# One weight unit for both gate rows in the last mixer, a third buffer for the mLSTM weights, and the order of its heads moved

## What is computed

```python
# x: 512 tokens, ctx: 256 tokens, D = 1024; 4 retention heads, 4 mLSTM heads of 128
hc = modulate(rms_norm(ctx, norm1), csh1, csc1)
rk_c, rv_c, mk_c, mv_c, gates_c = ...hc @ w_in...      # only states come out of the context
st_f, st_b = states after ctx, forward and backward
hx = modulate(rms_norm(x, norm1), sh1, sc1)
rq, rk, rv, rg, mq, mk, mv, mo, mg, bg_ret, bg_ml = split(hx @ w_in)
ret = retention(rope(rq), rope(rk), rv), forward + backward, from the states
ml  = mLSTM(mq, mk, mv, gates mg + bias), forward + backward, from the states
y_ret = head_norm(ret) * silu(rg);  y_ml = head_norm(sigmoid(mo) * ml)
x = x + g1 * ((sigmoid(bg_ret)*(y_ret @ w_ret_up) + sigmoid(bg_ml)*(y_ml @ w_ml_up)) @ w_out)
```

## Time and profile before

| | us |
|---|---|
| median of 3 runs (lowest, highest) | 2866.57 (2865.85, 2868.82) |
| profiled execution, device time | 2866.88 |
| profiled execution, span | 2865.2 |
| busy in the span: PE, DVE, ACT | 2807.3, 1457.5, 984.2 |

### The profile page before, as it was taken

The page is one execution under the profiler, slowest core; times in us unless marked ns, Lnnn a source line. Parts: engine busy times, 40 slices in busy tenths (PEclk is TensorE's granted clock), DMA queues, the critical chain, the costliest instruction groups (busy, mean ns, idle before and its releaser), DMA issues. The chain is left out here.

```text
span 2865.2 us, 34079 instructions
## 1 busy us (share of the span) xinstructions
PE 2807.3 (98%) x13630; PEld 2326.4 (81%) x13630; DVE 1457.5 (51%) x1931; ACT 984.2 (34%) x1093; POOL 32.9 (1%) x68
## 2 busy tenths in 40 slices
PE   7999999999999999999999999999999899899998
PEld 6888887788888888888887888888888788788886
DVE  7774356467743677434444443435545543623333
ACT  4222237432222322224444322324434432422221
POOL 0000000000000000000000000000000000000000
PEclk9999999999999999999999999999999999999999
DMA  5332231134322343222121322224311122222222
GB/s 182 136 139 88 103 134 60 45 134 148 136 103 103 125 140 138 95 107 92 49 74 45 118 89 102 88 103 147 110 70 65 45 74 103 74 102 92 98 103 74
DMA packets 68128, 288.80 MB, mean 101 GB/s; under 512 B 9488, under 2 KB 30352, under 8 KB 38464
## 3 DMA queue, kind: packets, MB, share of 16 engines
q1 hardware_dynamic: 59520, 257.97, 25.6%
q0 software_dynamic: 7936, 29.23, 3.0%
q10 hardware_dynamic: 576, 0.23, 0.0%
HBM read 285.31 MB, written 2.10 MB: 100 GB/s over the span
## 5 line engine op out<-in xcount | busy, mean ns | idle before, releaser
L1019 DVE TENSOR_TENSOR sb_WL<-sb_RAW,sb_WH 128x2048 fp32r<-128x2048 f32 x242 | 554.4, 2291 | 762.1 <-ACT sb_WH L435 761.9
L1797 PE MATMUL PS<-sb_HH,sb_WH 128*128 128x512 f32 x2288 | 900.8, 394 | 13.1 <-DVE sb_HL L1035 9.2
L1798 PE MATMUL PS<-sb_HL,sb_WH 128*128 128x512 f32 x2288 | 892.7, 390 | 0.0
L1799 PE MATMUL PS<-sb_HH,sb_WL 128*128 128x512 f32 x2288 | 892.6, 390 | 0.0
L435 ACT ACTIVATE sb_WH<-sb_RAW 128x2048 fp32r<-128x2048 f32 x242 | 463.2, 1914 | 788.5 <-PE PS L1799 786.6
L1797 PEld LDWEIGHTS PS<-sb_HH,sb_WH 128*128 128x128 f32 x2288 | 431.2, 188 | 107.9 <-issue 18.7
L1798 PEld LDWEIGHTS PS<-sb_HL,sb_WH 128*128 128x128 f32 x2288 | 431.1, 188 | 91.5 <-issue 3.4
L1799 PEld LDWEIGHTS PS<-sb_HH,sb_WL 128*128 128x128 f32 x2288 | 430.9, 188 | 90.5
L1797 PE MATMUL PS<-ff_GH,sb_WH 128*128 128x512 f32 x880 | 342.5, 389 | 1.9 <-DVE sb_WL L1019 1.9
L1798 PE MATMUL PS<-ff_GL,sb_WH 128*128 128x512 f32 x880 | 342.4, 389 | 0.0
L1799 PE MATMUL PS<-ff_GH,sb_WL 128*128 128x512 f32 x880 | 342.4, 389 | 0.0
(11 more groups left out here) (350 smaller groups left out, 2544.8 us busy)
## 6 DMA issues: line engine op xcount, KB each, us to landing
sb_RAW<-in_weights SPq DMA_DIRECT2D x230, 1024.0 KB, 4.8
ff_ADAW<-in_w_ada POOLq DMA_DIRECT2D x48, 512.0 KB, 4.0
sb_RAW<-in_weights SPq DMA_DIRECT2D x22, 512.0 KB, 5.1
sb_XT<-in_x SPq DMA_DIRECT2D x4, 512.0 KB, 9.7
out_t<-sb_XT SPq DMA_DIRECT2D x4, 512.0 KB, 2.7
b_CT<-in_ctx POOLq DMA_DIRECT2D x1, 1024.0 KB, 5.3
sb_RAW<-in_weights SPq DMA_DIRECT2D x4, 256.0 KB, 4.3
hy_BD<-in_c_gates POOLq DMA_DIRECT2D x1, 512.0 KB, 3.3
```

The lines of the kernel that those rows point to most:

```text
L1019: dve.tensor_tensor(WL[slot][:, :], RAW[slot][:, :], f32(WH[slot][:, :]), ALU.subtract).then_inc(*T["w_lo"].up())
L1797: pe.matmul(out, wh, xh, start=start, stop=False)
L1798: pe.matmul(out, wh, xl, start=False, stop=False)
L1799: return pe.matmul(out, wl, xh, start=False, stop=stop)
```

## The change

**Gates.** The unit with the gate columns is there once (242 used units instead of 243; the array in DRAM keeps its size). Its visit comes after the eight context visits and makes both rows: 24 matmuls of 256 columns on the context into one bank, 24 of 512 columns on the sequence into the next one. `take` moves both out with four ACT instructions. With that the context visits are the first of the list, the norm's steps begin one visit earlier (k = 0 to 3), and the visit in retention head 0 is gone; heads 1 to 3 keep theirs.

**mLSTM.** A third buffer `W2` lies over the gate rows, which are dead by then. d = 0 keeps `W0`, d = 1 uses `W1` and `W2` in turn. `weights(k)` waits for the values of k - 2 only for d = 0, for those of k - 4 for d = 1, and for the `QW` of k - 2. Both gate rows of the next head are spread together, ACT makes both sets of weights before it takes the visit out of PSUM, and DVE's list is ordered anew (below).

```diff
@@ lists
-    ("cmg", "cgates", 1), ("crk", "ctok", 2), ("crv", "ctok", 2), ("cmk", "ctok", 2), ("cmv", "ctok", 2),
-    ("rk", "feat", 2), ("rq", "feat", 2), ("rv", "tok", 2), ("mg", "gates", 1), ("mk", "feat", 2), ...
+    ("crk", "ctok", 2), ("crv", "ctok", 2), ("cmk", "ctok", 2), ("cmv", "ctok", 2), ("mg", "gates", 1),
+    ("rk", "feat", 2), ("rq", "feat", 2), ("rv", "tok", 2), ("mk", "feat", 2), ...
@@ buffers
-        WM = (ml["W0"], ml["W1"])
+        def WM(k):
+            return ml["W0"] if k % 2 == 0 else mz["W2"] if k % 4 == 3 else ml["W1"]
@@ ACT
             def weights(k):
                 ...
                 if k >= 2:
-                    act.wait_ge(T["ml_num"].sem, k - 1)
+                    act.wait_ge(T["ml_qw"].sem, k - 1)
+                    free = k - 1 if d == 0 else k - 3
+                    if free > 0:
+                        act.wait_ge(T["ml_num"].sem, free)
                 ...
             for h in range(NH):
                 if h + 1 < NH:
                     weights(2 * h + 2)
+                    weights(2 * h + 3)
+                    own_weights(2 * h + 2)
                 take(V_ML + h)
+                if h + 1 < NH:
+                    own_weights(2 * h + 3)
                 prepare(V_ML + h + 1)
                 if h + 1 < NH:
-                    weights(2 * h + 3)
                     squares(h)
@@ DVE
+            inter(0, 0)
             for h in range(NH):
+                inter(h, 1)
+                weighted(h, 0)
+                weighted(h, 1)
+                if h:
+                    gated_out(h - 1)
+                    prepare(V_ML + h)
+                weighted(h, 2)
+                weighted(h, 3)
                 if h:
                     head_sums(h - 1)
                 ...
                 divided(h, 0)
                 if h + 1 < NH:
                     own_keys(2 * h + 2)
+                    own_keys(2 * h + 3)
+                    inter(h + 1, 0)
                     divided(h, 1)
-                    own_keys(2 * h + 3)
-                    gated_out(h)
-                    prepare(V_ML + h + 1)
@@ PE, retention and mLSTM
             for h in range(NH):
                 ret_scores(h, 0)
                 ret_scores(h, 1)
-                visit(V_RET + h)
+                if h:
+                    visit(V_RET + h - 1)
                 ...
             for h in range(NH):
                 if h:
-                    spread(2 * h + 1)
                     part(V_ML + h, 0)
                 ...
                 if h + 1 < NH:
                     spread(2 * h + 2)
+                    spread(2 * h + 3)
```

More of the change, by code:

```diff
@@ L366, in _ @@
             u1 = U_B2 + len(B2_UNITS)
-            with sp.Fori(0, (N_UNITS - u1) // 2) as i:
+            with sp.Fori(0, (N_USED - u1) // 2) as i:
                 for s in range(2):
                     sp.wait_ge(T["w_lo"].sem, 2 * i + (u1 + s - 1))
-                    load((u1 + s) % 2, 2 * i + (u1 + s))
+                    load((u1 + s) % 2, 2 * i + (u1 + s + 1))
             for t in range(0, KT, 2):
@@ L540, in group @@
                     for c in range(chunks):
-                        if not isinstance(i, int) or ahead < u0 + chunks * (2 * i + j) + c + 1 < N_UNITS:
+                        if not isinstance(i, int) or ahead < u0 + chunks * (2 * i + j) + c + 1 < N_USED:
                             split_at(u0, 2 * chunks, i, chunks * j + c + 1)
@@ L840, in take @@
                             last.then_inc(*T["rope_sw"].up())
-                elif name in ("cmg", "mg"):
+                elif name == "mg":
                     act.wait_ge(T["mlb_in"].sem, 1)
-                    lo, w = (0, SC) if name == "cmg" else (SC, S)
-                    act.activation(gr["IG"][0:36, lo:lo + w], PS[0:36, b, 0:w], ACT.Identity, bias=col("ml_b", 0, rows=36))
-                    last = act.activation(gr["FG"][0:36, lo:lo + w], PS[64:100, b, 0:w], ACT.Identity, bias=col("ml_b", 1, rows=100)[64:100, :])
+                    for lo, w, bank_ in ((0, SC, b), (SC, S, b + 1)):
+                        act.activation(gr["IG"][0:36, lo:lo + w], PS[0:36, bank_, 0:w], ACT.Identity, bias=col("ml_b", 0, rows=36))
+                        last = act.activation(gr["FG"][0:36, lo:lo + w], PS[64:100, bank_, 0:w], ACT.Identity, bias=col("ml_b", 1, rows=100)[64:100, :])
                 elif name == "rg":
@@ L1686, in head_sums, with inter, weighted @@
                     .then_inc(*T["hn_ss"].up())
-            for h in range(NH):
[L1689 to L1696, removed]
+            def inter(h, d_):
+                dve.wait_ge(T["ml_w"].sem, 2 * h + d_ + 1)
+                if h:
+                    dve.wait_ge(T["ml_num"].sem, 2 * h + d_ - 1)
+                dve.tensor_tensor(mw["QW"][:, d_, :], b2["MQ"][:, h, :], SQT[:, d_, :], ALU.mult).then_inc(*T["ml_qw"].up())
+            def weighted(h, j):
+                dve.wait_ge(T["ml_s"].sem, TB * h + j + 1)
+                for d_ in range(2):
+                    lo, hi = span(d_, j)
+                    w = WM(2 * h + d_)
+                    last = dve.tensor_tensor(w[:, j, lo:hi], PS[:, j % 2, lo:hi], w[:, j, lo:hi], ALU.mult)
+                last.then_inc(*T["ml_sm"].up())
+            inter(0, 0)
+            for h in range(NH):
+                inter(h, 1)
+                weighted(h, 0)
+                weighted(h, 1)
+                if h:
+                    gated_out(h - 1)
+                    prepare(V_ML + h)
+                weighted(h, 2)
+                weighted(h, 3)
                 if h:
                     head_sums(h - 1)
[L1699 to L1703, removed]
-                        last = dve.tensor_tensor(WM[d_][:, j, lo:hi], PS[:, j % 2, lo:hi], WM[d_][:, j, lo:hi], ALU.mult)
-                    last.then_inc(*T["ml_sm"].up())
-                    if j == 1:
-                        inter(1)
                 dve.wait_ge(T["ml_qw"].sem, 2 * h + 2)
@@ L1908, in project @@
                 pe.wait_ge(T["w_lo"].sem, u + 1)
[L1909 to L1912 removed]
+                if kind == "feat":
+                    last = feature_major(u % 2, HH, HL, (b, b + 1), ready=ready)
+                elif kind == "gates":
+                    if u >= U_B2:
+                        feature_major(u % 2, hc["HCH"], hc["HCL"], (b,), tokens=SC)
+                        b += 1
+                    last = feature_major(u % 2, HH, HL, (b,), ready=ready)
                 elif kind == "tok":
@@ L2263, in ml_values @@
                     for j in order:
-                        last = pe.matmul(out, WM[d][:, j, c], b2["MV"][:, j, h, :], start=False, stop=j == order[-1])
+                        last = pe.matmul(out, WM(k)[:, j, c], b2["MV"][:, j, h, :], start=False, stop=j == order[-1])
                 last.then_inc(*T["ml_num"].up())
```

66 lines of the change are left out of this document (33 added, 33 removed).

## The result

The changed kernel takes 2850.88 us in the median of 5 runs (2849.65 to 2852.73), the kernel before beside it 2868.13 (2865.85 to 2868.82, 5 runs). The ratio is 0.9945, its 95% interval 0.9934 to 0.9956: 17 us less. The forecast was 2852.1 in a range of 2848.7 to 2858.1. The profiled execution took 2852.57, 14.3 less than the profiled one of before; the sum said 14.5 less.

What follows compares the result with a forecast made beforehand. PE was taken as the bound (98% of the span), with only its waits and the half clock behind some to gain. -6.8 + 3.3 + 1.7 + 0.7 - 13.4 = -14.5 gave 2852.4, forecast as a median of 2852.1, range 2848.7 to 2858.1.

Steps and rivals of the forecast that it cites:

- Start, -6.8: Start of the last mixer: PE's waits of 4.17 and 0.47 shrink or go, and the half clock goes; -6.8.
- the share of the clock: Start, second visit: 2.5 of the gain, as the clock should stay at its full level.
- Retention, the wait of 3.3: Retention head 0: without the gate visit PE waits for DVE's split and then its first score block; +3.3.
- Retention, 1.7 for the clock: Retention head 0: the half clock follows the new wait, as after two of three mLSTM waits; +1.7.
- the rival of the full clock: Retention head 0: the new wait keeps the full clock; 2850.4, chance 0.27.
- mLSTM, -13.4 and +0.7: mLSTM heads: three waits of 3.35 go (-10.0) with two half-clock stretches (-3.4); head 0's moved `QW` costs +0.7.
- the chain: mLSTM head 0 to 1: output done 2222.6, weighted blocks 2228.0, PE asks for them at 2229.3.
- The slack: mLSTM heads: time to spare before PE asks, 0.9 on ACT's output and 1.3 on DVE's weighted blocks.
- ACT's table load: mLSTM chain on ACT: load takes 1.28 without the skill's 1.38 drain; with the drain the sum would be -13.3.
- The slower rival: mLSTM heads: third buffer not free in time, PE waits 5.2 plus 1.7 for clock three times; 2872.8, chance 0.03.
- The sum: Whole profiled execution: all terms together -14.5, from 2866.88 to 2852.4.

Runs made afterwards that it cites:

- e3_scores_before_split: Changed kernel, but in retention head 0 DVE multiplies the first two blocks of scores before it splits the next unit; 2846.35 us, ratio 0.9928.
- e5_two_buffers_new_order: Changed kernel with two mLSTM weight buffers again and the new lists kept; 2875.11 us, ratio 1.0024.
- e7_one_more_act: Changed kernel with one more ACT `exp` of 0.7 us in the weights of d = 1, heads 1 to 3; 2852.35 us, ratio 0.9950.
- e6_third_buffer_old_order: Changed kernel's gates and three weight buffers, but the mLSTM lists of ACT, DVE and PE in the old order; 2865.30 us, ratio 0.9992.
- e7_three_more_act: Changed kernel with three more ACT `exp` (2.2 us) in the weights of d = 1, heads 1 to 3; 2854.50 us, ratio 0.9953.
- e9_filled_wait: Changed kernel with the second score product of retention head 0 made four times, so PE works in the wait; 2849.90 us, ratio 0.9940.
- e8_best: e3_scores_before_split with the second `QW` of mLSTM head 0 moved behind the first weighted block; 2847.23 us, ratio 0.9929.

## Why the prediction was right

- **Start, -6.8.** 6.9, the 7.0 of the table without the 0.1 from ahead of the mixer. All its times came within 0.4: norm 1961.05 for 1961.2, second visit 1962.22 for 1962.6, third 1968.29 for 1968.3. The 0.4 of waiting did not come, since DVE's split ended 0.4 earlier. Filling the idle time in the kernel before supports the share of the clock, in one profile.
- **Retention, the wait of 3.3.** 3.29 in its row, 3.45 by PE's starts (6.06 from the scores to the values, 2.61 in e3_scores_before_split), for the reason given, DVE's split ahead of the scores; moving the split behind them takes it away.
- **Retention, 1.7 for the clock.** The term that was mis-sized. In the profiled execution it is 2.8: from the values to the query times the state it is 8.21 after, 5.44 before. The 1.7 was read from mLSTM stretches at the low level of 3.4 us, and this one is 6.8 long, as were those of e5_two_buffers_new_order. A row of the length that was needed was at hand: the 4.17 at the start, with 2.5 behind it. And it comes in some executions only: by their times, not in two of the five runs, and perhaps not in the one at 2850.88.
- **Whether that loss comes at all.** The Trainium skill, page "TensorE: Matmul & The Clock Gate", section "HAM oscillation — how this bites in real kernels", tells of a kernel whose TensorE waits about 3 to 5 us for DMA at each turn of its loop, and falls to the low clock every time. Here the wait of 3.29 was followed by the low clock in four of six profiles, and not in those of e7_one_more_act and e6_third_buffer_old_order: at this length it is not certain. The forecast took the 1.7 in, and the median came out 1.2 under it, toward the rival of the full clock (2850.4), to which the three lowest of the five runs are nearer; the other two lie 0.5 and 0.6 over the forecast. The same kernel does both, so which of the two numbers the median comes near is luck.
- **mLSTM, -13.4 and +0.7.** 13.5 for the 12.7 forecast. The 0.7 is 0.73 in its row, 0.6 by PE's starts. A wait that goes takes a little more with it than the 3.35 of its row, for the reason read from e7_three_more_act: from spread to spread a head at the full clock took 25.25 before and takes 21.65. Each link of the chain held: output at 2222.1 for 2222.6, weighted blocks at 2227.5 for 2228.0, PE at 2229.17 for 2229.3. The slack was underrated, 1.2 for 0.9 on ACT, 1.6 for 1.3 on DVE, as the links came up to 0.5 earlier than reckoned.
- **ACT's table load.** The drain of 1.38 behind it that the Trainium skill states ("ScalarE: Activation LUTs", "What ACT_TABLE_LOAD costs") is not in this trace either: the `exp` before it ends at 2219.72, the load begins at 2219.74 and the output at 2221.03, 1.29 later. The measurement decides. No wait for the output came.
- **The slower rival** is real, 2875.11, and is not what the change does: the third buffer is free in time.
- **The sum**, 14.5 for 14.3 in the profiled executions, has errors that cancel, so that it came so near is in part luck: retention 1.2 too cheap, mLSTM 0.8 and the start 0.1 too modest, and 0.1 that is no part of the mixer. The medians differ by 17.2, since the profiled execution of after is one of its two at 2852.6, and that of before lies 1.3 under the median of the five runs beside it.

## What to carry to other kernels

When a stage is taken out or made shorter, look at the chain that ran beside it: the gate visit was cover for a split and a multiplication, and its removal gave back, as a wait and the low clock behind it, nearly all that the better start had won, until DVE's list was turned round. In a list that an engine runs in written order, the work that PE asks for next goes before work that has time. A further buffer and a new order may each be worth nothing or less alone: ask for each engine whether its first instruction is both the urgent one and free to start.

## What the runs showed of the hardware

- A wait of PE of 3.3 us brings the level of 1.2 GHz behind it in some executions of the same program and not in others: of the six profiles with the wait of 3.29 in retention, three have a stretch of 6.8 us, one of 3.4 and two none. With the wait filled, the four runs of e9_filled_wait lie within 0.5, those of the changed kernel within 3.1. It is not the only scatter: e3_scores_before_split and e8_best don't have that wait, and their runs lie within 1.7 and 1.4.
- What such a stretch costs goes with the time that PE works in it: 1.7 for one of 3.4 us, 2.5 to 2.9 for one of 6.8 that PE mostly works through, and 1.7 for one of 6.8 of which it works 3.9 (e5_two_buffers_new_order).
- Matmuls that nobody needs, made in a wait, went with the level of 2.4 GHz behind it in both profiles where that was tried, and delayed nothing: the values of retention started when DVE was done, and in the kernel before the visit behind the wait took 5.8 instead of 8.3, with 24 matmuls more. The median of that kernel is 2.1 lower, in an interval that holds no change. Why one wait of 3.3 is followed by the low level and another is not was not settled.
